# Overflow tables of a mixture of experts: one operand buffer or two in turn

## The reference, cut to what matters

```python
sel_idx = ...          # two experts for each token
gates = sel_vals / jnp.sum(sel_vals, axis=-1, keepdims=True)
counts = jnp.bincount(e_flat, length=N_EXPERTS)
...
def expert_block(args):
    xb, e = args
    a, g = jnp.split(xb @ w_up[e], 2, axis=-1)
    return (jax.nn.silu(g) * a) @ w_down[e]
...
out = jax.ops.segment_sum(ys * slot_gate[:, None], slot_tok, num_segments=T + 1)[:T]
```

## Time and profile before

| | |
|---|---|
| median of the runs | 1713.56 us (1712.64 to 1714.86) |
| profiled execution | 1712.22 us |
| its span, first to last instruction | 1710.6 us |
| busy: PE, DVE, ACT, POOL | 1594.7, 1180.2, 845.7, 201.6 us |
| mean granted clock of TensorE | 0.972 |
| expert stage | about 1040 to 1660 us of the span |
| HBM traffic over the span | 202 GB/s |

### The profile page before, as it was taken

The page is one execution under the profiler, slowest core; times in us unless marked ns, Lnnn a source line. Parts: engine busy times, 40 slices in busy tenths (PEclk is TensorE's granted clock), DMA queues, the critical chain, the costliest instruction groups (busy, mean ns, idle before and its releaser), DMA issues.

```text
span 1710.6 us, 20177 instructions
## 1 busy us (share of the span) xinstructions
PE 1594.7 (93%) x7701; PEld 1324.2 (77%) x7701; DVE 1180.2 (69%) x1472; ACT 845.7 (49%) x1140; POOL 201.6 (12%) x219
## 2 busy tenths in 40 slices
PE   6999999999999999999998986999988888899990
PEld 5788888888888888887887875888777777778870
DVE  3755867586666664422854775999888877889974
ACT  3013111216655564433301224788777777778875
POOL 0000000202222210000002220111111111111110
PEclk9999999999999999999999996999999999999995
DMA  5144536654244221412743576999999999999665
GB/s 156 41 94 57 128 69 84 83 111 121 67 110 126 76 63 56 141 48 58 244 129 117 185 260 228 356 372 380 351 348 339 338 330 338 332 342 375 221 221 205
DMA packets 156730, 329.27 MB, mean 192 GB/s; under 512 B 15664, under 2 KB 85296, under 8 KB 156635
## 3 DMA queue, kind: packets, MB, share of 16 engines
q1 hardware_dynamic: 140746, 289.69, 51.6%
q0 software_dynamic: 15888, 38.31, 7.8%
HBM read 296.74 MB, written 48.50 MB: 202 GB/s over the span
## 4 chain that ended last, share of the span: by engine, by line
PE 92%; DVE 3%; ACT 2%; DMA 1%; issue 1%; SPq 0%; DVEq 0%; POOLq 0%; ACTq 0%
PE ps L750 51%; PE ps L1045 31%; PE ps L851 2%; PE ps L836 2%; PE ps L1052 2%; DVE e_lo L1849 1%; PE ps L1058 1%; PE ps L993 1%; DMA x_raw<-in_x 1%; ACT zsq L1411 1%; ACT zsq L1407 0%; PE ps L981 0%; DMA z_d<-ye,row_i 0%; PE ps L767 0%; DMA xg<-x_d,tok_tab 0%
## 5 line engine op out<-in xcount | busy, mean ns | idle before, releaser
L1849 DVE TENSOR_TENSOR e_lo<-e_raw,e_hi 128x1024 fp32r<-128x1024 f32 x376 | 433.3, 1218 | 10.3 <-ACT e_hi L1348 6.0
L1348 ACT ACTIVATE e_hi<-e_raw 128x1024 fp32r<-128x1024 f32 x376 | 369.3, 1051 | 22.5 <-PE ps L1045 22.5
L750 PE MATMUL ps<-xt_hi,w_hi 128*128 128x512 f32 x896 | 303.3, 395 | 2.4 <-DVE xt_lo L1450 2.4
L750 PE MATMUL ps<-xt_lo,w_hi 128*128 128x512 f32 x896 | 299.1, 390 | 0.0
L750 PE MATMUL ps<-xt_hi,w_lo 128*128 128x512 f32 x896 | 298.9, 390 | 0.0
L1045 PE MATMUL ps<-e_hi,xe_hi 128*128 128x512 f32 x512 | 164.8, 403 | 39.6 <-DVE e_lo L1849 37.3
L750 PEld LDWEIGHTS ps<-xt_hi,w_lo 128*128 128x128 f32 x896 | 168.5, 188 | 36.0
L750 PEld LDWEIGHTS ps<-xt_hi,w_hi 128*128 128x128 f32 x896 | 168.3, 189 | 35.2 <-DVE xt_lo L1450 2.6
L750 PEld LDWEIGHTS ps<-xt_lo,w_hi 128*128 128x128 f32 x896 | 168.8, 188 | 33.0
L1483 DVE TENSOR_TENSOR w_lo<-w_raw,w_hi 128x512 fp32r<-128x512 f32 x136 | 94.9, 703 | 130.9 <-ACT w_hi L1123 127.5
L1123 ACT ACTIVATE w_hi<-w_raw 128x512 fp32r<-128x512 f32 x136 | 83.6, 628 | 202.1 <-PE ps L750 199.6
(11 more groups left out here) (276 smaller groups left out, 2268.4 us busy)
## 6 DMA issues: line engine op xcount, KB each, us to landing
e_raw<-in_w_up SPq DMA_DIRECT2D x128, 1024.0 KB, 11.0
e_raw<-in_w_down SPq DMA_DIRECT2D x64, 1024.0 KB, 11.6
w_raw<-in_w_in SPq DMA_DIRECT2D x64, 256.0 KB, 4.9
w_raw<-in_w_gate SPq DMA_DIRECT2D x48, 256.0 KB, 3.3
gates_d<-gate_t POOLq DMA_DIRECT2D x16, 512.0 KB, 3.3
gate_s<-gates_d SPq DMA_DIRECT2D x16, 512.0 KB, 3.6
qkv_d<-qkv POOLq DMA_DIRECT2D x12, 512.0 KB, 3.8
w_raw<-in_w_branch SPq DMA_DIRECT2D x24, 256.0 KB, 3.7
```

The costliest lines, as they stand in the source:

```text
L750: last = nc.tensor.matmul(o(h, c1 - c0), st(k), mv(k, c0, c1), start=start and k == nk[0] and n == 0, stop=h in stop and k == nk[-1] and n ...
L1348: nc.scalar.activation(e_hi[:, (UPT + s) % RSPL, :], e_raw[r][:, s % 2, :], ACT.Copy).then_inc(e_h, 1)
L1849: nc.vector.tensor_tensor(e_lo[:, sp_, :], e_raw[raw_slot(b, s)][:, s % 2, :], e_hi[:, sp_, :], ALU.subtract).then_inc(e_all, 1)
```

## The change

The two operands of an overflow matmul get a second buffer each. Piece i writes and `overflow_mm(i)` reads buffer i % 2, and piece i waits for `overflow_mm(i - 2)` (`o_tab` at i) in place of `overflow_mm(i - 1)` (`o_tab` at i + 1). The tiles move to places over `bmap` and `oh_base`.

```diff
-        by_rank_o = at("by_rank_o", [P, P], FP32, 142.75)
+        by_rank_o = at("by_rank_o", [P, 2, P], FP32, 140.75)
...
-        vals_o = at("vals_o", [P, 2, NOV], FP32, 143.75)
+        vals_o = at("vals_o", [P, 2, 2, NOV], FP32, 142)
...
             def overflow_mm(i):
                 pe.wait_ge(o_vals, i + 1)
-                nc.tensor.matmul(ps[:, 7, 10 * NE:10 * NE + 2 * NOV], by_rank_o[:], vals_o[:].rearrange("p c b -> p (c b)"),
+                nc.tensor.matmul(ps[:, 7, 10 * NE:10 * NE + 2 * NOV], by_rank_o[:, i % 2], vals_o[:, i % 2].rearrange("p c b -> p (c b)"),
                                  start=i == 0, stop=i == TOPK * TT - 1).then_inc(o_tab, 1)
...
                 k, t = i // TT, i % TT
-                if i > 0:
-                    dve.wait_ge(o_tab, i + 1)
-                go(V.tensor_scalar(by_rank_o[:], iota_p[:], rmod[:, k, t:t + 1], None, ALU.is_equal))
-                go(V.tensor_scalar(vals_o[:, 0], biota[:], blk_o[:, k, t:t + 1], tokm[:, t:t + 1], ALU.is_equal, ALU.mult))
-                go(V.tensor_scalar(vals_o[:, 1], biota[:], blk_o[:, k, t:t + 1], gates[:, k, t:t + 1], ALU.is_equal, ALU.mult))
+                if i > 1:
+                    dve.wait_ge(o_tab, i)
+                go(V.tensor_scalar(by_rank_o[:, i % 2], iota_p[:], rmod[:, k, t:t + 1], None, ALU.is_equal))
+                go(V.tensor_scalar(vals_o[:, i % 2, 0], biota[:], blk_o[:, k, t:t + 1], tokm[:, t:t + 1], ALU.is_equal, ALU.mult))
+                go(V.tensor_scalar(vals_o[:, i % 2, 1], biota[:], blk_o[:, k, t:t + 1], gates[:, k, t:t + 1], ALU.is_equal, ALU.mult))
                 wait_all()
                 dve.sem_inc(o_vals, 1)
```

## The result

The changed kernel takes 1686.66 us (median of four runs, 1685.78 to 1687.53) against 1713.19 for the kernel before in the same measurements: ratio 0.9844, 95% interval 0.9826 to 0.9861. That is 26.5 us less. The forecast was 1676.4, 36.8 us less, with a range up to 1685; so the direction was right, the size was not, and the range was missed by 1.7 us. The profiled execution took 1687.53 us.

What follows compares the result with a forecast made beforehand. PE was taken to bound the kernel, with 92% of the chain. The profiled 1712.22 us minus 37.2 for the expert stage, plus 0 for the fetches, gave 1675.0; 1.3 up to the median made 1676.4 us, range 1674 to 1685.

Steps and rivals of the forecast that it cites:

- The wait and the pauses: Expert stage, steps 8 to 24: DVE's 50.2 us wait for overflow matmuls and PE's 33.7 us for e_lo would go.
- PE's step of 18.01 us: Expert stage: a step with an overflow matmul but no pause takes PE 18.01 us, 0.28 of it for the matmul.
- The sum of 37.2 us: Expert stage, 16 steps from step 8: 287.88 us in place of 325.09, so 37.2 us less.
- DVE keeps up: Expert stage: DVE's step with a piece, 17.02 to 17.63 us, fits under PE's 18.01; cost nothing, at most 3.5 us.
- The fetches keep up: Weight fetches of the expert stage: 18.6 us a step by bytes, hidden by the reserve; cost 0, bounds 0 and 13 us.
- the bound of 13 us: Weight fetches: by landing times, 19.6 us a step, the landing time ends at 51 us, 13 over the lead.
- The reserve of 38 us: Weight buffers are refilled about 26 items, 38 us, before use; landing time would grow to 33 us, under that.
- Rival B: Fetches become the bound, ACT's e_hi waiting for e_raw in the last steps before the register loop: 1682 to 1689; chance 0.13.
- The rule of 358 GB/s: Weight fetches: 6.8 MB a step need 19.0 us, the reserve runs out by a microsecond or two, about 1678 us.
- C: Expert stage: DVE becomes the bound, at the upper value of its step; 1680 us, chance 0.02.
- D: Expert stage: the change fails and the wait still lasts to the end of PE's step; 1713.6 us, chance 0.02.
- E: Expert stage: the fetch queue stalls PE and its clock stays at 1.2 GHz; slower, five steps give 1753 us; chance 0.03.

Runs made afterwards that it cites:

- spread slots: Tokens of a block in the partitions whose bit 2 is 0, otherwise the same work: 1675.43 us from the kernel after, 1713.72 us from the kernel before.
- even slots: The kernel after with a block's tokens in the even partitions first (token r in partition 2r), otherwise the same work: 1673.44 us.
- 8 KB pieces: The kernel after with each partition's part of a weight fetch as one 8 KB run instead of two of 4 KB, transposes adapted: 1678.78 us.
- two variants: The kernel before with half of w_down's second pair left unfetched from block 9 on, 1714.36 us; and with tokens in partitions whose bit 2 is 0, 1713.72 us.

## Why the prediction was wrong, step by step

- **The wait and the pauses**: right. 50.2 us of DVE's wait went, 3.3 of PE's 33.7 are left from 1206 to 1536 us and lie behind 1474, the wait for matmul i - 2 never shows, the clock stayed at 1.00 in step 9.
- **PE's step of 18.01 us**, with 0.28 for the matmul: right, over 13 steps. **The sum of 37.2 us** is about what the edit is worth where nothing else intervenes: with spread slots and the same work the two kernels took 1713.72 and 1675.43 us, 38.3 apart, and in the profiled execution of the first the clock fell once more than in the kernel before, at 1.5 us.
- **DVE keeps up**: right; PE was busy 234.10 of 234.10 us with DVE at 218.73.
- **The fetches keep up**: this step failed. It said: "I take the bytes, since they count what was delivered over 71 and 70 us, while a landing time is the last of 16 engines' parts". This is the wrong way round. ACT waits for the last part, so the last part is what counts, and the mean over the engines hides it. The bytes gave 18.6 us for a step's fetches; measured were 19.4 (q1 from 1300 to 1474 us) and 19.1 (the steps from 24 on). The landing times, which I had put at the bound of 13 us, gave 19.6. Up to 1200 us an issue took SP 0.37 us, as nothing stopped it, so the engines that finished early could run ahead and lift the mean; that this is why the bytes read too high there is likely and not shown.
- **The reserve of 38 us**: half right. It held 13 steps, as the fetches lost some 1.5 us to PE in each: the smallest margin fell from 19.2 us in step 9 to 1.5 in step 21 and was gone in step 22; what ACT, DVE and PE had done ahead carried PE two steps further. I had the reserve last to the end.
- **Rival B**, with its place (ACT waiting for e_raw in the last steps before the loop) and its price (1682 to 1689), is what happened; it had a chance of 0.13 and belonged near one half, and the range should have reached its end. The rule of 358 GB/s for transfers between HBM and SBUF (the Trainium skill, SBUF — State Buffer, Summary: rules for kernel authors) lies close to the 353 and 355 GB/s that were moved, but the time that I worked out from it, 1678, is 9 us too low. As a limit it does not hold here: with the even slots q1 alone moved 355 GB/s and the core 388.
- **C, D and E** did not happen: no DVE bound, no old wait, and a granted clock of 1.00 from 1075 to 1636 us. The rows of 0.5 at the start of the stage, the last near 1068 us, stand in the kernel before as well (near 1066).

## What to carry to other kernels

When a stall goes, ask what had been resting meanwhile: here 2.4 us of pause a step hid a fetch queue that fell behind in every step without one. Judge such a queue by the arrival of its last part against the time of use, step by step, not by GB/s or by the DMA's share, which are both means over 16 engines. And look at which partitions small indirect DMAs touch: here a half-filled block in one half of the partitions made single parts of every fetch late, and renumbering its slots, with no other work, brought 1675 us (spread) and 1673 (even) for 1687.

## What the runs showed of the hardware

- The scatter and gather of some 64 rows of 4 KB in a step, 2.5 to 2.7 MB beside q1's 28 to 31 in 86 us, moved the last part of a 1 MB fetch from 7.3 to 22.7 us after its issue; in partitions chosen by bit 0 the same rows moved it to 11.5.
- With 4 KB pieces SP's queue took fetches some 22 us ahead of their landing (the median; 28 at most) and then stopped SP; with 8 KB pieces medians up to 32 us and single fetches up to 37 were seen.
- A pause of PE of 2.2 us was followed by a fall of the clock to 1.2 GHz once in the 15 pauses of the kernel before, and two and three times in the profiled executions of its two variants; each time cost 1.5 us.
- PE's plain step took 17.73 us in some profiled executions and 17.69 in others, with the same code of PE in it, at a granted clock of 1.00 throughout. This 0.2% is 1.2 us over 31 steps, and so a part of why the spread slots show 1675.4 and the even ones 1673.4.
